# Softplus without Abs, and the last two key blocks read by one strided matmul

## What is computed

```python
z = einsum("bhtd,bhsd->bhts", qb, kb) * scale
mask = s_idx < t_idx
log_keep = where(mask, log_sigmoid(-z), 0.0)          # = -softplus(z)
tail = cumsum(log_keep, axis=3, reverse=True)
between = concatenate([tail[..., 1:], zeros_like(tail[..., :1])], axis=-1)
a = where(mask, exp(log_sigmoid(z) + between), 0.0)
out = einsum("bhts,bhsd->bhtd", a, vb)
```

## Time and profile before

| | |
|---|---|
| time, median of 3 runs | 1585.61 us (1584.87 to 1587.32) |
| span of the profiled execution | 1583.1 us |
| median less span | 2.5 us |
| PE busy | 1542.2 us, 97% |
| DVE busy | 915.0 us, 58% |
| ACT busy | 645.1 us, 41% |
| POOL busy | 605.2 us, 38% |
| mean granted clock of PE | 0.988 |

### The profile page before, as it was taken

The page is one execution under the profiler, slowest core; times in us unless marked ns, Lnnn a source line. Parts: engine busy times, 40 slices in busy tenths (PEclk is TensorE's granted clock), DMA queues, the critical chain, the costliest instruction groups (busy, mean ns, idle before and its releaser), DMA issues. The chain is left out here.

```text
span 1583.1 us, 19904 instructions
## 1 busy us (share of the span) xinstructions
PE 1542.2 (97%) x6874; PEld 1262.7 (80%) x6874; DVE 915.0 (58%) x1217; ACT 645.1 (41%) x1027; POOL 605.2 (38%) x240
## 2 busy tenths in 40 slices
PE   8999999999999999998999999999999999999996
PEld 5777777778888888877888888888878888888874
DVE  6778787877777741158343342433677777730155
ACT  6677777433323322235353243432542332332232
POOL 3222223444444444433424334243344444444340
PEclk9999999999999999999999999999999999999998
DMA  4111201223222332223223222122222322332221
GB/s 168 42 54 40 66 13 67 77 98 103 94 93 98 103 135 92 76 81 131 81 67 101 86 80 93 66 93 93 68 92 96 103 93 93 108 123 95 86 80 54
DMA packets 37193, 137.78 MB, mean 87 GB/s; under 512 B 4128, under 2 KB 4256, under 8 KB 37024
## 3 DMA queue, kind: packets, MB, share of 16 engines
q1 hardware_dynamic: 36576, 134.61, 25.4%
q10 hardware_dynamic: 576, 2.62, 0.4%
HBM read 135.12 MB, written 2.10 MB: 87 GB/s over the span
## 5 line engine op out<-in xcount | busy, mean ns | idle before, releaser
L306 POOL TENSOR_TENSOR wl<-raw,wh 128x1024 fp32r<-128x1024 f32 (+1 forms) x236 | 605.0, 2568 | 943.5 <-ACT wh L1086 943.3
L331 PE MATMUL bank<-xh,wh 128*128 128x512 f32 x1280 | 504.3, 394 | 7.4 <-DVE xl L720 7.3
L334 PE MATMUL bank<-xl,wh 128*128 128x512 f32 x1280 | 500.8, 391 | 0.0
L335 PE MATMUL bank<-xh,wl 128*128 128x512 f32 x1280 | 500.1, 391 | 0.0
L1086 ACT ACTIVATE wh<-raw 128x1024 fp32r<-128x1024 f32 (+1 forms) x236 | 258.7, 1099 | 437.1 <-PE bank L331 385.9
L331 PEld LDWEIGHTS bank<-xh,wh 128*128 128x128 f32 x1280 | 241.9, 189 | 60.3 <-DVE xl L720 10.6
L335 PEld LDWEIGHTS bank<-xh,wl 128*128 128x128 f32 x1280 | 241.8, 189 | 51.0
L334 PEld LDWEIGHTS bank<-xl,wh 128*128 128x128 f32 x1280 | 241.9, 189 | 49.2 <-issue 0.2
L734 DVE TENSOR_TENSOR x<-x,bank 128x512 f32<-128x512 f32 x56 | 38.2, 682 | 234.4 <-PE bank L335 234.4
L899 DVE SCALAR_TENSOR_TENSOR conv<-gate,par,conv 128x512 f32<-128x512 f32 x88 | 150.3, 1708 | 14.7 <-DVE conv L895 6.5
L331 PE MATMUL bank<-yh,wh 128*128 128x512 f32 x352 | 136.9, 389 | 0.0
(11 more groups left out here) (173 smaller groups left out, 1966.9 us busy)
## 6 DMA issues: line engine op xcount, KB each, us to landing
raw<-in_w SPq DMA_DIRECT2D x204, 512.0 KB, 3.3
raw<-in_w SPq DMA_DIRECT2D x32, 704.0 KB, 4.0
x<-in_xT SPq DMA_DIRECT2D x8, 256.0 KB, 5.4
outT<-x SPq DMA_DIRECT2D x8, 256.0 KB, 2.2
pin<-in_pT ACTq DMA_DIRECT2D x2, 512.0 KB, 5.2
decay<-in_consts ACTq DMA_DIRECT2D x1, 1024.0 KB, 6.0
rotary<-in_consts ACTq DMA_DIRECT2D x1, 512.0 KB, 3.9
cst<-in_consts SPq DMA_DIRECT2D x1, 256.0 KB, 7.1
```

What stands on the lines that cost most here:

```text
L306: nc.gpsimd.tensor_tensor(wl[:, slot, cols], raw_slot(ATT_RING if like < ATT_TILES else RAW_RING, r, blocks), wh[:, slot, cols].bitcast(F3 ...
L331: first = mm(out, ah_, bh_, start=start, stop=False, skip_group_check=True)
L334: mm(out, ah_, bl_, start=False, stop=False, skip_group_check=True)
L335: return mm(out, al_, bh_, start=False, stop=stop, skip_group_check=True)
```

## The change

Softplus was max(z, 0) + ln(1 + exp(-|z|)), with Abs, Exp and Ln on ACT. It becomes max(z, min(ln(1 + exp(z)), 20)), with Exp straight from `Z` and Ln on ACT; DVE's instruction keeps its size and its place. The two copies into `both_h` and `both_l` go: `sph` and `spl` of block 2 are made 512 columns wide, the high and low part of `both` are written at columns 256 to 383 of them, and the matmul reads columns 0 to 127 and 256 to 383 as two pieces.

```diff
-            both_h, both_l = sb("both_h", [2, P], F32R, ph), sb("both_l", [2, P], F32R, ph)
+            both_h, both_l = sph[TB - 2][:, 2 * P:3 * P], spl[TB - 2][:, 2 * P:3 * P]
...
                     if j == TB - 3:
                         pe.wait_ge(both_low, s + 1)
-                        pe.wait_ge(both_copied, 2 * s + 2)
...
                         if j < j2 == TB - 2:
-                            parts = (both_h[:].rearrange("p a t -> p (a t)"), both_l[:].rearrange("p a t -> p (a t)"))
+                            out = out.rearrange("p (a t) -> p a t", t=P)
+                            parts = [part[j2][:].rearrange("p (a t) -> p a t", t=2 * P)[:, :, 0:P] for part in (sph, spl)]
...
-                    vec.scalar_tensor_tensor(sp[j][:], Z[j][:, 0:T - j * P], 0.0, sp[j][:], ALU.max, ALU.add)\
+                    vec.scalar_tensor_tensor(sp[j][:], sp[j][:], SOFTPLUS_LINEAR, Z[j][:, 0:T - j * P], ALU.min, ALU.max)\
...
-                def magnitude(jj):
+                def exponential(jj):
                     j = TB - 1 - jj
                     act.wait_ge(z_done, 4 * s + jj + 1)
-                    nc.scalar.activation(sp[j][:], Z[j][:, 0:T - j * P], ACT.Abs).then_inc(z_abs, 1)
-
-                def exp_negative(jj):
-                    j = TB - 1 - jj
-                    act.wait_ge(z_abs, 4 * s + jj + 1)
-                    nc.scalar.activation(sp[j][:], sp[j][:], ACT.Exp, scale=-1.0).then_inc(z_exp, 1)
+                    nc.scalar.activation(sp[j][:], Z[j][:, 0:T - j * P], ACT.Exp).then_inc(z_exp, 1)
...
-                steps = (magnitude, exp_negative, ln_one_plus)
-                for t in range(TB + 2):
-                    for k, step in enumerate(steps):
-                        if 0 <= t - k < TB:
-                            step(t - k)
-                act.wait_ge(sp_low, 4 * s + 2)
-                for both_, part in ((both_h, sph), (both_l, spl)):
-                    copy(both_[:, 0, :], part[TB - 2][:, 0:P].bitcast(F32), both_copied)
+                for t in range(TB + 1):
+                    if t < TB:
+                        exponential(t)
+                    if t:
+                        ln_one_plus(t - 1)
```

More of the change, by code:

```diff
@@ L44 @@
 MASKED = -1e30
+SOFTPLUS_LINEAR = 20.0
 NORMS = 7
@@ L131, in program @@
             sp = [sb(f"sp{j}", [T - j * P], F32, ph) for j in range(TB)]
-            sph = [sb(f"sph{j}", [T - j * P], F32R, ph) for j in range(TB)]
-            spl = [sb(f"spl{j}", [T - j * P], F32R, ph) for j in range(TB)]
+            sph = [sb(f"sph{j}", [T if j == TB - 2 else T - j * P], F32R, ph) for j in range(TB)]
+            spl = [sb(f"spl{j}", [T if j == TB - 2 else T - j * P], F32R, ph) for j in range(TB)]
             both = sb("both", [P], F32, ph)
-            both_h, both_l = sb("both_h", [2, P], F32R, ph), sb("both_l", [2, P], F32R, ph)
+            both_h, both_l = sph[TB - 2][:, 2 * P:3 * P], spl[TB - 2][:, 2 * P:3 * P]
             ah = [sb(f"ah{j}", [T - j * P], F32R, ph) for j in range(TB)]
@@ L188, in program @@
         qk_high, q_moved, qk_low, vt_high = (sem(n) for n in ("qk_high", "q_moved", "qk_low", "vt_high"))
-        z_done, z_abs, z_exp, z_ln = sem("z_done"), sem("z_abs"), sem("z_exp"), sem("z_ln")
+        z_done, z_exp, z_ln = sem("z_done"), sem("z_exp"), sem("z_ln")
         sp_full, sp_high, sp_low = sem("sp_full"), sem("sp_high"), sem("sp_low")
-        both_full, both_high, both_low, both_copied = (
-            sem(n) for n in ("both_full", "both_high", "both_low", "both_copied"))
+        both_full, both_high, both_low = (sem(n) for n in ("both_full", "both_high", "both_low"))
         cum_done, a_full, a_high, a_low = sem("cum_done"), sem("a_full"), sem("a_high"), sem("a_low")
@@ L402, in cumulate @@
                         pe.wait_ge(both_low, s + 1)
-                        pe.wait_ge(both_copied, 2 * s + 2)
                     for j2 in range(j, TB if j == TB - 2 else max(j + 1, TB - 1)):
                         left = negtri if j2 == j else negones
-                        parts = (sph[j2][:], spl[j2][:])
+                        out = Z[j][:, (j2 - j) * P:T - j * P]
+                        parts = (sph[j2][:, 0:T - j2 * P], spl[j2][:, 0:T - j2 * P])
                         if j < j2 == TB - 2:
-                            parts = (both_h[:].rearrange("p a t -> p (a t)"), both_l[:].rearrange("p a t -> p (a t)"))
+                            out = out.rearrange("p (a t) -> p a t", t=P)
+                            parts = [part[j2][:].rearrange("p (a t) -> p a t", t=2 * P)[:, :, 0:P] for part in (sph, spl)]
                         for part in parts:
-                            last = mm(Z[j][:, (j2 - j) * P:T - j * P], left[:], part, start=False,
-                                      stop=True, skip_group_check=True)
+                            last = mm(out, left[:], part, start=False, stop=True, skip_group_check=True)
                     last.then_inc(cum_done, 1)
@@ L818, in softplus_high @@
                     dve.wait_ge(sp_full, 4 * s + jj + 1)
-                    vec.tensor_copy(sph[j][:], sp[j][:]).then_inc(sp_high, 1)
+                    vec.tensor_copy(sph[j][:, 0:T - j * P], sp[j][:]).then_inc(sp_high, 1)
                 def softplus_low(jj):
@@ L823, in softplus_low @@
                     dve.wait_ge(sp_high, 4 * s + jj + 1)
-                    low(spl[j][:], sp[j][:], sph[j][:], sp_low)
+                    cols = slice(0, T - j * P)
+                    low(spl[j][:, cols], sp[j][:], sph[j][:, cols], sp_low)
                 def last_two():
@@ L829, in last_two @@
                     dve.wait_ge(both_full, s + 1)
-                    vec.tensor_copy(both_h[:, 1, :], both[:]).then_inc(both_high, 1)
+                    vec.tensor_copy(both_h, both[:]).then_inc(both_high, 1)
                     dve.wait_ge(both_high, s + 1)
-                    low(both_l[:, 1, :], both[:], both_h[:, 1, :], both_low)
+                    low(both_l, both[:], both_h, both_low)
                 def weights_low(jj):
```

## The result

The changed kernel takes 1592.86 us (median of 14 runs, 1586.70 to 1595.33), the kernel before 1585.37 in the same comparison. The ratio is 1.0046, with a 95% interval of 1.0038 to 1.0054: 0.46% slower, where 1592.6 was forecast. The profiled execution has a span of 1592.9 us (before 1583.1).

The account below looks back on a forecast made before the run. PE was taken to bound the kernel, busy 97% of the span. Pair delays of 4.9 and 0.5 us and 1.6 for the clock made 7.0: span 1590.1, plus 2.5 to the median, 1592.6 us; range 1576 to 1602.

Parts of the forecast that it names:

- What sets the pair's length: Attention: the end of block 4's low part in half 1 sets the 31.61 us pair length, one for one.
- Half 0: Attention, half 0: POOL comes earlier, block 4's low part ends at 141.9 instead of 140.53; 0.6 us of cover hides it.
- Half 1: Attention, half 1: POOL's two turns delay softplus; block 4's low part ends at 158.75 instead of 157.94, +0.8 us per pair.
- The sum: Whole kernel: 4.9 us for six pairs, 0.5 for the first, 1.6 for the clock; 7.0 us in all.
- one more fall of the clock: PE in the attention: one more drop from 2.4 to 1.2 GHz, costing 1.6 us.
- The signs of being wrong: POOL's turn on another instruction, more than four clock falls in attention, or L410 in two pieces longer than 0.28 us.
- The two pieces: PE's matmul reading 256 columns in two pieces: cost taken as 0, up to 7 us kept for the range.
- The faster rival: Half 1: POOL's second turn stays out or comes later, PE's waits go; 8 to 13 us less, chance 0.23.
- The slower rival: POOL 0.2 us earlier in half 0, so half 1 loses 1.4 to 2.0 us per pair; about 1599, chance 0.22.

Follow-up runs that it names:

- strided_only: The changed kernel with the old softplus (Abs, Exp, Ln) back: no two copies, matmul in two pieces; 1609.62 us, 1.0164 of the kernel before.
- early_tiles: The kernel before with only ACT's weight tiles moved right behind the last Ln, ahead of the copies; 1600.81 us, 1.0099 of the kernel before.
- softplus_only: The kernel before with only the new softplus; the two copies, their wait and the one-piece matmul stay; 1574.41 us, 0.9928 of the kernel before.
- hold_both: The changed kernel plus an ACT wait for the low part of `both` behind the last Ln; 1574.65 us, 0.9933 of the kernel before.
- hold_block3: The changed kernel plus an ACT wait for the low part of block 3 behind the last Ln; 1574.39 us, 0.9928 of the kernel before.
- hold_half0: The changed kernel plus an ACT wait for the low part of block 3, in half 0 of each pair alone; 1593.95 us, 1.0053 of the kernel before.
- the held versions: The changed kernel with one more wait on ACT; for example hold_both took 1574.65 us and hold_block3 1574.39 us.
- hold_block2: The changed kernel plus an ACT wait for the low part of block 2 behind the last Ln; 1595.06 us, 1.0063 of the kernel before.

## Why the prediction was right, point by point

*What sets the pair's length.* It was said that the end of the low part of block 4 in half 1 does, one for one, 4.73 us before the next pair. After the change it is 98.89 - 94.16 = 4.73 us. In strided_only and early_tiles it is 4.7 too (34.3 - 29.6 and 34.0 - 29.3), and it still is where PE no longer waits before block 4: 30.33 - 25.61 = 4.72 in softplus_only, 30.47 - 25.75 in hold_both. PE's own pace is not reached there; by the rows of softplus_only it would be some 30.1 us (124.37 - 94.26). The rule ends where POOL's turn falls on the low part of the weights, ahead of that of k: in hold_block3 the distance is 7.07.

*Half 0.* In the profile, counted from the start of the pair, POOL starts 6.90 us into the pair (73.39), laid out 6.9 (138.0 - 131.06); the low part of block 3 ends at 9.72 (76.21), laid out 9.7; the low part of block 4 ends at 10.78, laid out 10.8; `take_qk` starts at 11.30, laid out 11.3. No wait of PE came of it. In the six pairs in which the clock had fallen, POOL's turn came later against DVE: in four it hit the low part of block 4 (2.77 at 175.16, POOL from 174.74), in two the high part of block 4 (2.63 at 242.62, POOL from 242.54). That was not laid out. It had no effect in the pair's length that the rows show: the 1.5 us between 33.9 and 32.4 is what a fall costs before the change too (33.2 and 31.6).

*Half 1.* Laid out: softplus from 149.6, POOL at 152.7, low part of block 4 at 158.75. Measured, on the same clock: 149.65, 152.65 and 158.73. Both of POOL's turns fell where forecast. hold_half0 shows that they would have done so without the delay from half 0; the text had given half 0 a share in it, by way of DVE's later start. That start turned out to change nothing, since POOL was ahead of the low part of block 3 in either case.

*The sum.* 0.82 us per pair was forecast for six pairs and is 0.79 (where no fall adds to it); 0.5 for the first pair, and is 0.2; one more fall of the clock, and in the profile there are three more. This last term was the badly sized one, 1.6 us against 4.6 in that execution. The median's 7.5 us, less the 5.0 us of waits, leaves some 2.5 for the clock, which is an inference and not a row: the runs spread from a span of 1584.9 at a mean clock of 0.991 to 1593.5 at 0.986. How often the clock falls differs from run to run, and the forecast had only its range for that. The 2.5 us between span and median hold the 1.8 to 1.9 us by which each run of either kernel is longer than its own span; the rest says only that the profiled run of the kernel before was faster than the median. The collision was worked out. That the whole comes so close, 7.0 us forecast against 7.5, is in part luck: the first pair was put too high and the clock too low, and the profiled execution by itself is 9.8 us longer.

*The signs of being wrong.* Two of the three that the prediction named did show. The clock fell more often than four times in attention, and in half 0 POOL's turn fell on another instruction in six pairs. Neither touches the collision of half 1, which is the same in all seven pairs that have it. The third, a longer L410 in two pieces, did not show.

*The two pieces.* 0 was taken, up to 7 kept for the range; the rows of 128x256 show 0.

*The faster rival* had the right size for what the softplus is worth: 8 to 13 us less were named, 11 came in softplus_only and in the held versions. It needed POOL's second turn not to get in between, or POOL to come later; POOL did get in. *The slower rival* turned on 0.2 us in half 0, and that margin held. The copy of block 3 started at 6.46 us into the pair (72.95), laid out at 6.7, and POOL at 6.90: 0.44 us behind it. early_tiles shows the other side of it: in half 0 of the pair from 68.59 POOL starts at 75.50, 0.09 us ahead of the high part of block 3, which takes 2.55, and in half 1 0.08 us ahead of it (91.52 and 91.60).

The Trainium skill's rule in "SBUF — State Buffer", section "Who interferes with whom", was that the second of the two to issue fully blocks until the first is done. By that rule the trace agrees in the softplus rows shown of these kernels, with 2.60 for a copy of 0.42 in the change; the rule says what an overlap costs, and the place of the overlap had to come from the rows.

## What to carry to other kernels

An engine that is not on the critical path can still be timed right: the two copies, which looked like 0.6 us of waste, held back the work of a third engine so that it hit one instruction of softplus and not two. Before taking a wait away from such an engine, list what is queued behind it, and on whose instructions that will fall. When a removal loses, put the wait back without the work: here that one line makes 18 us of difference at one place in ACT's order of waits, and none to the good at the place just before.

## What was not expected of the hardware

The edge between two outcomes is narrow, and the same from pair to pair. In hold_block2 POOL's instruction starts 0.08 us behind one of DVE's that reads two SBUF tiles, which keeps its own length; in hold_both it starts 0.05 us ahead of one (87.36 and 87.41), and that one takes 2.90. With 0.02 us and less between the recorded starts either can happen, as two rows of the trace of before show. POOL starts at 311.14, 0.02 us ahead of the first, and at 1375.41, 0.01 us ahead of the second:

```profile
311.16 0.68 DVE L714 TENSOR_TENSOR sumsq<-sumsq,square 128x512 f32<-128x512 f32 x1
...
1375.42 3.76 DVE L899 SCALAR_TENSOR_TENSOR conv<-gate,par,conv 128x512 f32<-128x512 f32 x1 [0.27 <-DVE conv L895]
```

The first keeps its own length; the second takes 3.0 us longer than the shortest of its kind (0.75). In the first case DVE's instruction before it still ran when POOL came. So the prediction's reading, that POOL goes next where it already waits, holds in the rows of softplus, where POOL came 0.05 us and more ahead of DVE's next, and not in this one with 0.02.

In the change the clock of TensorE fell although PE had no idle time over 1.3 us in these pairs: what it did just before was 0.6 us of waiting and then the twelve short score matmuls. The falls came more often in the change (six pairs in a row in the profile, against three), and with the shorter pairs of softplus_only there was one in the attention, at 188 us. But the length of the pair does not decide it: behind the first pair, early_tiles with its 34.0 us has one fall, at 199 us and not at the scores but in a wait of 2.1 us in `cumulate`, and hold_half0 with the same 32.4 us as the change has two, at 69 and 264 us. Why they came in each pair of this execution was not tested and stays open.
